# Products of the next head pair in 18 slots instead of 27, with ScalarE's and Pool's order changed to suit

## The reference

```python
def stick_breaking(q, k, v, bias, q_pos, k_pos):
    z = jnp.einsum('nqhd,nkhd->nhqk', q, k) * (C_HEAD_DIM ** -0.5) + bias
    mask = (k_pos[None, :] < q_pos[:, None])[None, None]
    log_beta = jax.nn.log_sigmoid(z)
    log_1m = jnp.where(mask, jax.nn.log_sigmoid(-z), 0.0)
    rest = lax.cumsum(log_1m, axis=3, reverse=True) - log_1m
    w = jnp.where(mask, jnp.exp(log_beta + rest), 0.0)
    return jnp.einsum('nhqk,nkhd->nqhd', w, v)
```

## Time and profile before

| | us |
|---|---|
| median of 3 runs | 3218.91 |
| the profiled execution | 3217.85 |
| its span | 3216.1 |
| TensorE matmul busy | 2987.0 (93%) |
| VectorE, ScalarE, Pool busy | 1599.6, 979.1, 1183.8 |
| the attention loop, first to last slot | 1478.1 to 2274.9 |

### The profile page before, as it was taken

One profiled execution on the slowest core, in us unless ns is written; L12 is line 12 of the kernel. 1 busy time (PEld: TensorE's weight loads), 2 busy tenths in 40 slices (PEclk: granted clock), 3 DMA queues, 4 the chain that ended last, 5 costly groups with the idle time before them and its releaser, 6 DMA issues.

```text
span 3216.1 us, 53131 instructions
## 1 busy us (share of the span) xinstructions
PE 2987.0 (93%) x20056; PEld 2795.6 (87%) x20056; DVE 1599.6 (50%) x2285; ACT 979.1 (30%) x1946; POOL 1183.8 (37%) x836
## 2 busy tenths in 40 slices
PE   6999987999999999988899888987889999999997
PEld 6999976899999999976777777775789999999995
DVE  3565566833332213385777666667683332221336
ACT  2334321211001001044767667676321100100102
POOL 4222221133333333314546455454213333333330
PEclk9999988999999999998999999998899999999998
DMA  3111110233434343314444444444111111111111
GB/s 97 41 40 41 40 34 27 85 121 125 149 121 150 125 149 124 107 44 127 124 112 119 123 119 123 116 119 118 37 33 46 46 46 42 47 46 42 46 44 55
DMA packets 380991, 269.41 MB, mean 84 GB/s; under 512 B 12452, under 2 KB 376689, under 8 KB 378804
## 3 DMA queue, kind: packets, MB, share of 16 engines
q1 hardware_dynamic: 371764, 263.03, 27.2%
q10 hardware_dynamic: 9088, 4.52, 0.5%
HBM read 243.71 MB, written 82.51 MB: 101 GB/s over the span
## 4 chain that ended last, share of the span: by engine, by line
PE 79%; DVE 8%; POOL 4%; ACT 3%; issue 3%; DMA 2%; SPq 1%; DVEq 0%; ACTq 0%; POOLq 0%
PE bank L1660 61%; PE bank L1809 5%; POOL E L747 2%; PE bank L1883 2%; DVE L L1440 2%; PE bank L1903 1%; DMA PK<-k_by_sample 1%; PE bank L1824 1%; PE bank L1683 1%; PE bank L1873 1%; DVE R L1547 1%; PE bank L1916 1%; ACT L L985 1%; PE bank L1861 1%; DVE KT L1278 1%
## 5 line engine op out<-in xcount | busy, mean ns | idle before, releaser
L1660 PE MATMUL bank<-XH,WH 128*128 128x352 f32 x2688 | 879.6, 327 | 18.4 <-DVE XL L1560 7.1
L1660 PE MATMUL bank<-XH,WL 128*128 128x352 f32 x2688 | 867.1, 323 | 0.0
L1660 PE MATMUL bank<-XL,WH 128*128 128x352 f32 x2688 | 866.9, 323 | 0.0
L683 POOL TENSOR_TENSOR WH<-RAW,zero 128x1024 fp32r<-128x1024 f32 (+1 forms) x170 | 317.5, 1868 | 1484.8 <-PE bank L1660 1483.5
L1660 PEld LDWEIGHTS bank<-XH,WH 128*128 128x128 f32 x2688 | 509.2, 189 | 23.1 <-issue 19.4
L1660 PEld LDWEIGHTS bank<-XH,WL 128*128 128x128 f32 x2688 | 510.3, 190 | 0.5
L1660 PEld LDWEIGHTS bank<-XL,WH 128*128 128x128 f32 x2688 | 508.1, 189 | 0.0
L1660 PE MATMUL bank<-HH,WH 128*128 128x352 f32 x1440 | 469.1, 326 | 26.8 <-DVE HL L1388 17.0
L1660 PE MATMUL bank<-HH,WL 128*128 128x352 f32 x1440 | 466.4, 324 | 0.0
L1660 PE MATMUL bank<-HL,WH 128*128 128x352 f32 x1440 | 466.0, 324 | 0.0
L1599 DVE TENSOR_TENSOR HF<-SG,bank 128x352 f32<-128x352 f32 x132 | 68.6, 521 | 721.3 <-PE bank L1660 712.9
(11 more groups left out here) (275 smaller groups left out, 4227.8 us busy)
## 6 DMA issues: line engine op xcount, KB each, us to landing
k_by_sample<-in_cache_k_dram SPq DMA_DIRECT2D x64, 512.0 KB, 5.0
v_by_sample<-in_cache_v_dram SPq DMA_DIRECT2D x64, 512.0 KB, 5.7
PK<-k_by_sample SPq DMA_DIRECT2D x128, 256.0 KB, 3.0
PV<-v_by_sample SPq DMA_DIRECT2D x128, 256.0 KB, 4.7
RAW<-in_ffn_w_gate_dram SPq DMA_DIRECT2D x44, 512.0 KB, 3.8
RAW<-in_ffn_w_up_dram SPq DMA_DIRECT2D x44, 512.0 KB, 3.8
RAW<-in_ffn_w_down_dram SPq DMA_DIRECT2D x32, 512.0 KB, 4.0
RAW<-in_ab_w_in_dram SPq DMA_DIRECT2D x24, 512.0 KB, 3.8
```

Of the source, the lines that this page charges most:

```text
L683: nc.gpsimd.tensor_tensor(WH[slot][:, 0:kb, :], RAW[slot][:, 0:kb, :], zero[:].to_broadcast([P, kb, P]), ALU.add).then_inc(w_split, 1)
L1660: last = t.matmul(to[:, 0:CW], w[slot][:, k, :], x[:, k, CH[c]], start=n == 0, stop=n == 3 * kb - 1)
```

## The change

A product is cut in two halves of twelve matmuls instead of three thirds, and these lie in the 18 slots of a list (0, 1, 3, 5, 7, 9, 10, 13, 14, 15, 18, 19, 20, 22, 24, 26, 27, 29), in the same order of products. In a slot with a first half TensorE does the turns that are due ahead of the wait and the half; in all others after the product, as before. ScalarE empties the staging bank right after the decay, ahead of outputs and turned weights. Pool splits a tile in eight eighths (one block of 128 each) in slots 0 to 7, 11 to 18 and 20 to 27; the counts of its semaphore follow. The two tiles that are split ahead of the loop are split in eighths too.

```diff
-PIECES = 3
-PIECE_FROM = 3
+PIECES = 2
+PIECE_SLOTS = [0, 1, 3, 5, 7, 9, 10, 13, 14, 15, 18, 19, 20, 22, 24, 26, 27, 29]
...
-    u, piece = divmod(s - PIECE_FROM, PIECES)
-    if not 0 <= u < 9:
+    if s not in PIECE_SLOTS:
         return None
+    u, piece = divmod(PIECE_SLOTS.index(s), PIECES)
...
-                    m, k = n0 + 3 * hp + j, slice(2 * part, 2 * part + 2)
+                    m, k = n0 + 3 * hp + j, slice(part, part + 1)
...
-                for part in range(4):
+                for part in range(8):
                     split_part(0, 2, part)
...
-                    if 3 <= s < 7:
-                        split_part(hp + 1, 1, s - 3)
-                    if 12 <= s < 16 and hp < NPAIR - 1:
-                        split_part(hp + 1, 2, s - 12)
-                    if 21 <= s < 25 and hp < NPAIR - 1:
-                        split_part(hp + 2, 0, s - 21)
+                    if s < 8:
+                        split_part(hp + 1, 1, s)
+                    if 11 <= s < 19 and hp < NPAIR - 1:
+                        split_part(hp + 1, 2, s - 11)
+                    if 20 <= s < 28 and hp < NPAIR - 1:
+                        split_part(hp + 2, 0, s - 20)
...
                         decayed(at + 1)
+                    if 1 <= at <= NSEG:
+                        hb, sb = divmod(at - 1, PER_PAIR)
+                        piece = piece_at(sb)
+                        if hb < NPAIR - 1 and piece and piece[2] == PIECES - 1:
+                            take_product(hb + 1, *piece[:2], banks[6])
                     if 0 <= at - 2:
                         output(at - 2)
...
-                            piece = piece_at(sb)
-                            if piece and piece[2] == PIECES - 1:
-                                take_product(hb + 1, *piece[:2], banks[6])
...
+                    if piece and piece[2] == 0:
+                        turns()
+                        pe.wait_ge(p_ev, unit_of(hp + 1, *piece[:2]))
+                    if piece:
                         product_c(hp + 1, *piece[:2], banks[6], piece[2])
...
+                    if not piece or piece[2]:
+                        turns()
```

More of the change, by code:

```diff
@@ L715, in split_part @@
                         pool.wait_ge(d_mm, 3 * n0 + unit_of(0, "q", 2) + 5 if m == n0 + 2 else 3 * m + 1)
-                    nc.gpsimd.tensor_tensor(WH[s][:, k, :], RAW[s][:, k, :], zero[:].to_broadcast([P, 2, P]),
+                    nc.gpsimd.tensor_tensor(WH[s][:, k, :], RAW[s][:, k, :], zero[:].to_broadcast([P, 1, P]),
                                             ALU.add).then_inc(w_part, 1)
-                    pool.wait_ge(w_part, 4 * (3 * hp + j - 2) + part + 1)
+                    pool.wait_ge(w_part, 8 * (3 * hp + j - 2) + part + 1)
                     rest = nc.gpsimd.tensor_tensor(WL[s][:, k, :], RAW[s][:, k, :], WH[s][:, k, :].bitcast(F32),
                                                    ALU.subtract)
-                    if part == 3:
+                    if part == 7:
                         rest.then_inc(w_split, 2)
@@ L1943, in attention_pe, with turns @@
                         continue
[L1944 to L1947, removed]
-                        product_c(hp + 1, *piece[:2], banks[6], piece[2])
[L1949 to L1955, removed]
+                    piece = piece_at(s) if hp < NPAIR - 1 else None
+                    def turns():
+                        for what, p, n in turns_at(hp, s):
+                            if what == "page":
+                                turn_pages(p, n)
+                            elif what == "out":
+                                turn_output(p, n)
+                            else:
+                                turn_tokens(what, p, n)
+                    if piece and piece[2] == 0:
+                        turns()
+                        pe.wait_ge(p_ev, unit_of(hp + 1, *piece[:2]))
+                    if piece:
+                        product_c(hp + 1, *piece[:2], banks[6], piece[2])
+                    if not piece or piece[2]:
+                        turns()
             def mean(n, c):
```

## The result

The changed kernel takes 3182.57 us, median of four runs (3179.26 to 3191.85), beside 3218.61 for the kernel before in the same runs: a ratio of 0.9891, 95% interval 0.987 to 0.9913. The profiled execution has a span of 3180.6 us, 35.5 under the 3216.1 of before; the forecast was 51.0. Two single executions of kernels further down took 5198.79 and 7383.24 us, far from all others of the same kernels, and are left out of the medians given there. The first windows are cut at the head pairs: length, then busy us of each engine, clock, DMA.

What follows compares the result with a forecast made beforehand. Pairs were held to lose time because TensorE's work and the chain beside it don't meet slot by slot. Per pair 5.6 - 10.4 - 1.1 - 1.6 = -7.5 us; seven pairs -52.5, start +1.5: 3166.9 us, range 3147 to 3206.

Steps and rivals of the forecast that it cites:

- Switches: TensorE's products in a pair: 27 thirds of 1.40 us become 18 halves of 2.03; counted as -1.1 us a pair.
- Products in slots 0 and 1: Halves there remove waits at slots 1, 2 and 21; the clock no longer falls, -1.6 us a pair.
- ScalarE empties the staging bank first: TensorE's waits for the staging bank at unit boundaries fall from 2.8 us a pair to about 0.4.
- Pool's eighths: Pool's weight splits: 24 eighths at an assumed 1.0 us replace 12 quarters of 1.72; some 3.4 us more, costing nothing by itself.
- Rival A: VectorE and Pool collisions keep the pair's waits at 10.0 us: -3.1 a pair, 3199 us; chance 0.16.
- New waits: Waits left in a pair: Pool's product 2.55 us, key page 1.9, others and collisions; 5.6 in place of 10.4.
- Rival D: The clock falls instead behind slots 11 and 12, and 16 and 17: 3.2 us a pair, 3190 us; chance 0.03.
- Once, at the start: Ahead of the loop, eight more Pool instructions make TensorE's 3.50 us wait for the first split 1.5 longer.

Runs made afterwards that it cites:

- the first experiment: The changed kernel with TensorE doing the turns of every slot behind the product again, as before the change: 3183.52 us, ratio 0.9898.
- the last two: Kernel with two pages first, plus ScalarE emptying the bank before the decay at pair boundaries and copying value tokens first: in halves 3145.01 us, in thirds 3142.7.
- the mended kernel: The changed kernel with turns ahead only in slots 10, 14 and 27, one key page's load first, and the first two tiles split whole: 3160.36 us, 0.9819.
- the kernel with two pages first: The kernel with three costs undone, but SyncE issues two key pages, not one, ahead of the store of keys and value pages: 3149.37 us, 0.9786.

## Why the prediction was right, and where its terms were not

The direction, the mechanism and the place were right: the pairs lost time because work and chain did not meet, and filling slots 0 and 1 and freeing the staging bank gave it back. The size was 15.5 us too large (51.0 for 35.5), and that it was not further off is in part luck, as two waits that were reckoned too long (2.3 us a pair, for Pool and the page) stand against one that was not reckoned at all (3.7). By its steps:

- *Switches* and *Products in slots 0 and 1*: busy time was to fall by 2.7 us a pair; it fell by 3.2 to 3.4 where the clock held (91.66 to 88.42 and 88.24). The clock's part, taken as 1.6, is 2.0 to 2.2 by the thirds from slot 0 (91.66 to 89.51 in the last of the pairs); it was read from one pair, whose fall lasted 3.4 us, and in the last three of the seven it lasted 6.8. The switches', taken as 1.1, is 0.3 to 0.6 between halves and thirds in otherwise like kernels (88.88 and 89.17 in the first experiment and the one with thirds, 88.2 and 88.8 in the last two). The half microsecond or more that is left of the fall was not traced. The waits at slots 1 and 21 went.
- *ScalarE empties the staging bank first*: 2.8 to 0.4 was forecast, and 0.8 came. The four neighbouring boundaries that were counted have no row; the fifth, from slot 29 to slot 0 of the next pair, was not counted, and all 0.8 is there.
- *Pool's eighths*: 1.34 us for an assumed 1.0, inside the bounds of 0.92 to 1.72. Pool is busy for 66 us a pair in place of 55, and its product of weights is waited for less all the same: the run with quarters has 10.8 us more of these waits, and 9 us more in the loop. Rival A, for which these waits had to stay near 38 us, falls with their 11.6.
- *New waits* is the step that was mis-sized: 5.6 us a pair for 7.4 (52.0 / 7). Pool's product was overcounted, 2.55 for 1.7 (11.6 / 7): waits came at slots 13, 19 and 20, 9.1 us in the seven pairs, with 2.6 once where the loop starts, and none at slots 22 to 26, for which 1.45 a pair was reckoned. In part this is the turn bank, which now holds TensorE up at slots 3, 7 and 24 and gives the chain its time. With the turns behind, Pool's waits are 2.5 (17.3 / 7), but that this is the forecast's number is luck: slots 22, 24 and 25 still have none, slot 26 has 0.33, and slots 4, 5 and 8 make up the rest. The key page was overcounted too, 1.9 for 0.5; with the turns behind it is 2.2, as reckoned. What the step did not have is the 3.7 us (25.7 / 7) of turns moved in front of the half, which wait for one bank that is emptied behind other work. The step followed each engine's queue to Pool's product, and not the turns, which it treated as work without a wait of their own.
- A fall of the clock in slot 24 of two pairs, behind this wait, and another in slot 0, were not in the sum. The two pairs are 98.70 and 98.90 us beside 95.1, 7.4 together. Rival D had falls at slots 11 and 16, and none came there.
- *Once, at the start*: 1.5 was forecast and 3.1 came (6.62 for 3.50). The fixed part of an instruction was reckoned from Pool working alone; there it shares the time with VectorE (rows in the last section). The loop started another 1.8 us later, for something upstream of the stage: Pool's clearing of a buffer ahead of it began as much later (1436.71 for 1434.92) in this execution.

Together: the waits fell 10 us less than forecast (33.6 forecast, 23.4 in the rows of both kernels, small rows taken in), the busy time 2 less (18.9 for 16.8), and the start cost 3.4 more (4.9 for 1.5).

## What to carry to other kernels

When work is moved ahead of a wait, it brings its own waits to the front: ask of the moved instruction who empties its destination and what stands ahead of that on the emptying engine. A wait taken away shows the next one, here the turn bank, then the page, then the next page in the same queue: to put the turns back gained nothing by itself, with one page's load first as well it was 9 us under the changed kernel, and in the mended kernel the second page's load first gave 11 more. Cut an instruction finely where its engine must answer something urgent in between, and leave it whole where someone waits for its end.

## What the runs showed of the hardware

Pool's splits and VectorE's subtractions of two operands did not run side by side. Ahead of the loop an eighth's instruction took 0.62 to 0.78 us while VectorE worked (all but the first) and 0.40 to 0.45 when it had stopped:

```profile
1444.74 0.78 POOL L719 TENSOR_TENSOR WL<-RAW,WH 128x128 fp32r<-128x128 f32 x1
...
1450.00 0.45 POOL L719 TENSOR_TENSOR WL<-RAW,WH 128x128 fp32r<-128x128 f32 x1
```

With whole splits (the mended kernel) it is VectorE that pays; first two subtractions alone (x2, 1.05 us together), then the two beside the two instructions of Pool shown above, one by one:

```profile
1443.06 1.05 DVE L1413 TENSOR_TENSOR QS<-QF,QS 64x352 fp32r<-64x352 f32 x2
1444.14 2.13 DVE L1415 TENSOR_TENSOR KSL<-KF,KSH 64x352 fp32r<-64x352 f32 x1
1446.29 2.61 DVE L1415 TENSOR_TENSOR KSL<-KF,KSH 64x352 fp32r<-64x352 f32 x1
```

Each of the two ended 0.38 us after the instruction of Pool beside it (1446.27 after 1445.89, 1448.90 after 1448.52). Read so, the engines take turns by whole instructions, and every cut of Pool's work lets one more of VectorE's through ahead of it. The Trainium skill ("SBUF — State Buffer", Who interferes with whom) says that a VectorE instruction with two inputs in SBUF contends with a Pool instruction that reads SBUF; these rows agree.

That is not the whole price of the eighths at the start. Alone, a quarter's pair of instructions goes out every 1.38 us in the kernel before (1449.43 to 1450.81), an eighth's every 0.89 in the changed one (1449.52 to 1450.41):

```profile
1449.43 0.61 POOL L716 TENSOR_TENSOR WH<-RAW,zero 128x256 fp32r<-128x256 f32 x1
1450.13 0.73 POOL L719 TENSOR_TENSOR WL<-RAW,WH 128x256 fp32r<-128x256 f32 x1
```

By these a tile would take 5.5 us in quarters and 7.1 in eighths, an estimate: 1.6 of the 3.1 us is the fixed part of eight more instructions, as forecast, and the rest fits the turns with VectorE.

The clock fell to 0.50 (1.2 GHz) behind a stretch in which TensorE was busy for 2.25 of 4.10 us, in slot 24 of the seventh pair:

```profile
2136.00:2140.10 4.10, 2.25 (x19) 2.10 (x18) 3.99 (x7) 3.68 (x10) 3.70 (x5) 1.00 0.14 32
2140.10:2143.50 3.40, 3.40 (x15) 3.34 (x14) 1.53 (x3) 0.57 (x3) 3.08 (x6) 0.50 0.69 185
```

The same wait of 1.87 us stood in slot 24 of the fourth pair without a fall (95.10 us at 1.00). What decides between them these runs don't settle; they show that the falls were fewer where the long waits were gone: none behind the loop's start in the seven pairs of the kernel with two pages first.
